# Recurrent stage of a two-block layer: modulation weights in quarter slots with three buffers, and two of the dense weight loads asked for at other places

## What is computed

```
sh1, sc1, ga1, sh2, sc2, ga2 = adaln(c, w_mod[i], b_mod[i])        # silu(c) @ w_mod + b
px = modulate(rms_norm(x, norm_mix[i]), sh1, sc1) @ w_in[i]
pc = modulate(rms_norm(xc, norm_mix[i]), csh1, csc1) @ w_in[i]
yc_rw, s_ctx = rwkv_mix(rwkv_streams(conv3(pc[..., :RW_COLS], ...)), (s_zero, s_zero), ...)
yx_rw, _ = rwkv_mix(rwkv_streams(conv3(px[..., :RW_COLS], ...)), s_ctx, ...)
yx = concat([yx_rw, short_conv_mix(px, ...), fourier_mix(px)]) @ w_out[i]
```

## Time and profile before

| | us |
|---|---|
| median of 3 runs | 3565.4 |
| lowest and highest | 3557.53, 3569.54 |
| the profiled execution, its time | 3560.43 |
| the profiled execution, its span | 3558.3 |
| PE busy | 3416.1 (96%) |
| DVE busy | 2336.2 (66%) |
| ACT busy | 564.6 (16%) |

### The profile page before, as it was taken

One profiled execution on the slowest core, in us unless ns is written; L12 is line 12 of the kernel. 1 busy time (PEld: TensorE's weight loads), 2 busy tenths in 40 slices (PEclk: granted clock), 3 DMA queues, 4 the chain that ended last, 5 costly groups with the idle time before them and its releaser, 6 DMA issues. The chain is left out here.

```text
span 3558.3 us, 58548 instructions
## 1 busy us (share of the span) xinstructions
PE 3416.1 (96%) x25037; PEld 2754.3 (77%) x25037; DVE 2336.2 (66%) x4471; ACT 564.6 (16%) x1072; POOL 162.9 (5%) x168
## 2 busy tenths in 40 slices
PE   7998899999999999999999999999999999999999
PEld 4455565577778888889998866767877888888888
DVE  2377777885559888998777654555754656644644
ACT  2232222221010000000003133222221000000000
POOL 1000000000000000000001000000001000000000
PEclk9999999999999999999999999999999999999999
DMA  9833323353686888776674734544324676654543
GB/s 338 259 91 100 103 81 106 106 140 105 210 284 223 260 260 260 244 245 204 196 232 160 229 125 142 166 142 157 103 73 148 221 233 201 222 174 161 178 166 130
DMA packets 663410, 638.48 MB, mean 179 GB/s; under 512 B 43490, under 2 KB 630752, under 8 KB 662128
## 3 DMA queue, kind: packets, MB, share of 16 engines
q1 hardware_dynamic: 554464, 563.16, 49.3%
q10 hardware_dynamic: 108016, 71.44, 6.9%
q0 software_dynamic: 672, 0.15, 0.0%
HBM read 628.41 MB, written 6.29 MB: 178 GB/s over the span
## 5 line engine op out<-in xcount | busy, mean ns | idle before, releaser
L2005 PE MATMUL bank<-work,extra 128*128 128x256 f32 x2112 | 463.0, 379 | 0.0
L664 DVE SCALAR_TENSOR_TENSOR work<-weight_ring,silu_c,work 128x256 f32<-128x256 f32 x1050 | 450.5, 502 | 0.0
L2005 PEld LDWEIGHTS bank<-work,extra 128*128 128x128 f32 x2112 | 400.7, 190 | 54.1
L2005 PE MATMUL bank<-weight_ring,work 128*128 128x256 f32 x1408 | 316.7, 383 | 7.8 <-ACT work L2138 7.5
L2206 DVE TENSOR_TENSOR work<-weight_ring 128x2048 f32<-128x2048 f32 (+2 forms) x72 | 129.6, 1800 | 293.1 <-DMA weight_ring<-in_w_gate_up 168.2
L2005 PEld LDWEIGHTS bank<-weight_ring,work 128*128 128x128 f32 x1408 | 268.4, 192 | 45.3 <-issue 8.3
L1013 PE MATMUL bank<-work,x_channels 128*128 128x256 f32 (+1 forms) x704 | 243.5, 486 | 0.0
L2752 PE MATMUL bank<-work,weight_ring 128*128 128x512 f32 x448 | 203.9, 600 | 1.2 <-PEq L2448 1.2
L1013 PEld LDWEIGHTS bank<-work,x_channels 128*128 128x128 f32 x704 | 129.3, 194 | 75.6 <-issue 63.5
L2005 PE MATMUL bank<-weight_ring,extra 128*128 128x256 f32 x704 | 159.4, 379 | 3.5 <-DVE extra L2201 3.5
L2005 PE MATMUL bank<-work 128*128 128x256 f32 x704 | 159.2, 379 | 0.0
(11 more groups left out here) (463 smaller groups left out, 5477.9 us busy)
## 6 DMA issues: line engine op xcount, KB each, us to landing
weight_ring<-in_w_mod SPq DMA_DIRECT2D x80, 2048.0 KB, 9.9
weight_ring<-in_w_gate_up SPq DMA_DIRECT2D x44, 2048.0 KB, 9.3
weight_ring<-in_w_in SPq DMA_DIRECT2D x26, 2048.0 KB, 9.5
weight_ring<-in_w_gate SPq DMA_DIRECT2D x22, 2048.0 KB, 8.3
weight_ring<-in_w_up SPq DMA_DIRECT2D x22, 2048.0 KB, 13.3
weight_ring<-in_w_down SPq DMA_DIRECT2D x20, 2048.0 KB, 8.1
weight_ring<-in_w_mod ACTq DMA_DIRECT2D x32, 1024.0 KB, 6.4
weight_ring<-in_w_out SPq DMA_DIRECT2D x16, 2048.0 KB, 9.6
```

Source lines behind the costliest of these rows:

```text
L664: ins = v_.scalar_tensor_tensor(a, w[:, k, :], c, a, ALU.mult, ALU.add)
L2005: last = mm(product(u, p), right[p][:, k, :], left[p][:, k, :], start=k == 0, stop=k == 7)
```

## The change

- The one buffer `mod_half` (8 steps) becomes three buffers `mod_part` of 4 steps (512 KB): two in the place of the old one, the third in the tile `work`. `load_part(n)` asks for a quarter slot as soon as DVE is done with the part three before it. A unit has eight parts. ACT asks for parts 2 and 3 of a unit after it has taken out x0, part 4 after the decays, part 5 after the last solve result (`w_out`), 6 and 7 after PE's `read_rows`, and the next unit's 0 and 1 at the end of the unit.
- The dense weights that ACT asked for after `w_out` (by the first `dense_out` behind it) are asked for before the `w_out` copies, inside the solve.
- `dense_out` at the first place of the chain (`marks[hp, 0]`, `n == 0`) no longer asks for weights. ACT then waits for `r_mm` (the end of `read_rows`) and asks for them there, ahead of parts 6 and 7.

```
-    mod_half = take("slot2", 2048).rearrange("p (k c) -> p k c", k=KT // 2)
+    mod_part = [take("slot2", 4, 256) for _ in range(2)]
...
+    mod_part.append(take("work", 4, 256))
...
-            def dense_out(upto):
+            def dense_out(upto, fetch=True):
...
-                    load(LOADS_UPTO[j + 1] + WBUFS)
+                    if fetch:
+                        load(LOADS_UPTO[j + 1] + WBUFS)
...
-            def load_half(n):
-                W("mod_step", KT // 2 * n)
-                c0 = (MOD_FIRST + n // 2) * 256
-                act.dma_start(mod_half, st.dram["w_mod"][n % 2 * 1024:n % 2 * 1024 + 1024, c0:c0 + 256].rearrange("(t p) n -> p t n", p=P)
-                              ).then_inc(S("mod_half_in"), 16)
+            def load_part(n):
+                W("mod_step", 4 * (n - 2))
+                k0, c0 = n % 4 * 4 * P, (MOD_FIRST + n // 4) * 256
+                act.dma_start(mod_part[n % 3], st.dram["w_mod"][k0:k0 + 4 * P, c0:c0 + 256].rearrange("(t p) n -> p t n", p=P)
+                              ).then_inc(S(f"mod_in{n % 3}"), 16)
...
-                load_half(4 * hp + 1)
+                load_part(8 * hp + 2)
+                load_part(8 * hp + 3)
...
+                load_part(8 * hp + 4)
                 if hp:
                     squares(hp - 1)
...
                 dense_out(marks[hp, "round"] - 1)
+                W("dense_mm", marks[hp, "round"])
+                load(LOADS_UPTO[marks[hp, "round"]] + WBUFS)
                 for tp in range(2):
                     W("w_mm", 2 * hp + tp + 1)
...
-                load_half(4 * hp + 2)
+                load_part(8 * hp + 5)
                 dense_out(marks[hp, "gram"])
                 for n in range(14):
-                    dense_out(marks[hp, n])
-                    if n == 1:
-                        load_half(4 * hp + 3)
+                    dense_out(marks[hp, n], n > 0)
+                    if n == 0:
+                        W("r_mm", hp + 1)
+                        load(LOADS_UPTO[n_out] + WBUFS)
+                        load_part(8 * hp + 6)
+                        load_part(8 * hp + 7)
                 dense_out(marks[hp, "end"])
                 if more:
-                    load_half(4 * hp + 4)
+                    load_part(8 * hp + 8)
+                    load_part(8 * hp + 9)
```

More of the change, by code:

```diff
@@ L1398, in dense_out @@
                     n_out += 1
-            def load_half(n):
-                W("mod_step", KT // 2 * n)
-                c0 = (MOD_FIRST + n // 2) * 256
-                act.dma_start(mod_half, st.dram["w_mod"][n % 2 * 1024:n % 2 * 1024 + 1024, c0:c0 + 256].rearrange("(t p) n -> p t n", p=P)
-                              ).then_inc(S("mod_half_in"), 16)
+            def load_part(n):
[3 more added lines that the diff above has]
+                              ).then_inc(S(f"mod_in{n % 3}"), 16)
             load(WBUFS)
-            load_half(0)
+            load_part(0)
+            load_part(1)
             def key_squares(hp):
@@ L1662, in head_norm, with mod_macs @@
                 v_.tensor_tensor(st.yr[:, hp, :], bank[4][:, T:2 * T], yn, ALU.mult).then_inc(S("y_gated"), 1)
-            def mod_macs(half, steps):
-                slot = half // 2
-                acc = mod_acc[:, slot % MOD_GROUP, :]
+            def mod_macs(part, steps=range(4)):
+                acc = mod_acc[:, part // 4 % MOD_GROUP, :]
                 if 0 in steps:
-                    W("mod_half_in", 16 * (half + 1))
+                    W(f"mod_in{part % 3}", 16 * (part // 3 + 1))
                 for k in steps:
-                    kc = half % 2 * (KT // 2) + k
+                    kc = part % 4 * 4 + k
                     x = st.silu_c[:, kc:kc + 1]
                     if kc == 0:
-                        ins = v_.tensor_scalar(acc, mod_half[:, k, :], x, None, ALU.mult)
+                        ins = v_.tensor_scalar(acc, mod_part[part % 3][:, k, :], x, None, ALU.mult)
                     else:
-                        W("mod_step", half * (KT // 2) + k)
-                        ins = v_.scalar_tensor_tensor(acc, mod_half[:, k, :], x, acc, ALU.mult, ALU.add)
+                        W("mod_step", 4 * part + k)
+                        ins = v_.scalar_tensor_tensor(acc, mod_part[part % 3][:, k, :], x, acc, ALU.mult, ALU.add)
                     ins.then_inc(S("mod_step"), 1)
-            whole = range(KT // 2)
             unit_keys(0)
@@ L1693, in _ @@
                     W("dense_mm", DENSE.index(("modsum", hp - 1)) + 1)
-                mod_macs(4 * hp, whole)
+                mod_macs(8 * hp)
+                mod_macs(8 * hp + 1)
                 W("gr_mm", hp + 1)
@@ L1707, in _ @@
                         v_.tensor_tensor(x, bank[tp + 2 * d][:].rearrange("p (a b) -> p a b", a=4), x, ALU.add).then_inc(S("z_add"), 1)
-                mod_macs(4 * hp + 1, whole)
+                mod_macs(8 * hp + 2)
+                mod_macs(8 * hp + 3)
                 if more:
@@ L1725, in _ @@
                     if tp == 0:
-                        mod_macs(4 * hp + 2, whole)
+                        mod_macs(8 * hp + 4)
+                        mod_macs(8 * hp + 5)
                 W("r_mm", hp + 1)
@@ L1740, in _ @@
                     if n in MOD_CHAIN:
-                        mod_macs(4 * hp + 3, range(n - MOD_CHAIN[0], n - MOD_CHAIN[0] + 1))
+                        i = n - MOD_CHAIN[0]
+                        mod_macs(8 * hp + 6 + i // 4, range(i % 4, i % 4 + 1))
                     if n >= 2:
```

## The result

| | before | after |
|---|---|---|
| median of 20 runs each, us | 3564.94 | 3575.50 |
| lowest and highest, us | 3557.53, 3584.53 | 3561.72, 3587.53 |
| profiled execution: its time, its span, us | 3560.43, 3558.3 | 3578.16, 3576.4 |
| mean granted clock of the profiled execution | 0.987 | 0.981 |

The ratio after to before is 1.0025, with an interval from 1.0016 to 1.0034: the changed kernel is 10.6 us slower by its medians, 17.7 us by the two profiled executions. The forecast was 3560 us.

The account below looks back on a forecast made before the run. The prediction took PE, the busiest engine, to bound the kernel, so only its stand-stills could come back. Terms of -11.8, +8.5 and 0 summed to -3.3 us, set against a mean of 3563.2: 3560 us, eight-in-ten range 3545 to 3574.

Parts of the forecast that it names:

- What bounds the kernel, and what "issue" is: PE is busiest, so only its stand-stills can come back; "issue" gaps in the transitions are each one late instruction packet.
- the smallest gap that the prediction took: Transitions: 1.9 us taken to stay of a gap, since matmuls use up a packet faster than one is fetched.
- Part 1: Transitions of units 0 to 6: less load there shortens PE's gaps and a wait for ACT, -11.8 us.
- the danger that was named with 0 to 1 us: The load in the solve can delay the packet fetched just before the transitions, 0 to 1 us a unit, 0 taken.
- The upper bound of part 1: All gaps of units 0 to 6 to zero, 17.7 us with the ACT wait.
- Part 2: Chain step 6, units 1 to 5: modulation parts land later behind two dense loads, +8.5 us (5.0 to 11.5).
- the two ways of reckoning: Landing of unit 2's chain part, at 3.5 or 4.4 us per further MB: 473.8 or 475.1.
- Part 3: The rest: five more DMA issues a unit on ACT, four-step slots, dense loads moved; 0, at most 3 us in all.
- PE already waits there, so it is lost one for one: Chain step 6: each microsecond of longer wait costs PE one, 1.7 us a unit in five units.
- The parts come in time: Faster rival, chance 0.27: parts land before chain step 6, DVE's and PE's waits go, -19.5 us, 3544 us.
- The burst decides (slower): Slower rival, chance 0.14: chain loads land in turn, +3.6 us a unit, part 1 halved, 3575; decides from 2.3 a unit.
- The fetches are late all the same: Rival, chance 0.05: SP's small blocks keep the transition gaps, sum +8.5 us at most, 3571 us.

Follow-up runs that it names:

- sp_later: parts_first with SP's stream of the next stage's weights started behind PE's first transition half of unit 7; 3536.41 us, ratio 0.9925.
- sp_after_both: parts_first with SP's stream of the next stage's weights started behind PE's second transition half of unit 7; 3532.53 us, ratio 0.9903.
- quarters_only: The changed kernel with the dense loads where they were before, so the quarter slots alone; 3553.09 us, ratio 0.9974.
- no_solve_load: The changed kernel without the dense load inside the solve, which goes back to the first dense_out behind w_out; 3575.76 us, ratio 1.0037.
- parts_no_solve: parts_first without the dense load inside the solve, which goes back to the first dense_out behind w_out; 3545.02 us, ratio 0.9943.
- dense_only: The kernel before with the two dense loads moved as in the change and the halves of modulation weights kept; 3584.10 us, ratio 1.0064.
- dose_one_12: parts_first with twelve small DVE operations added at chain step 6 of units 0 to 5, no DMA changed; 3578.04 us, ratio 1.0044.
- parts_first: The changed kernel with parts 6 and 7 asked for ahead of the dense loads behind the read rows; 3535.73 us, ratio 0.9927.
- the first experiments: quarters_only, dense_only, no_solve_load and parts_first, beside which the kernel before had a median of 3563.36 us.
- dose_one_6: parts_first with six small DVE operations added at chain step 6 of units 0 to 5, no DMA changed; 3545.84 us, ratio 0.9951.

## Why the prediction was wrong

**What bounds the kernel, and what "issue" is: right.** The gaps went where the load went, in the changed kernel and in sp_later and sp_after_both. In unit 2 of the changed kernel the packet of the instruction queue is seen once between 444.2 and 445.5, and PE goes on at 446.56, again some 1.3 us after its end:

```profile
q1 hardware_dynamic: 500, 0.03, 30.8%
q8 instruction: 1, 0.02, 4.5%
```

No packet of q10 is in this stretch, and still 1.99 us are lost: the smallest gap that the prediction took, 1.9, was the right size (1.93 to 1.99 in units 1, 2, 3 and 6, 1.70 in unit 5).

**Part 1, -11.8: the terms right within 0.5 us, the sum less.** Unit 2: 3.05 and 2.44 (3.1 and 2.4 predicted); unit 3: 2.91 (2.9); unit 1: 0.55 (0.6); unit 6: 0.82 (0.9); unit 0: 1.59 for the gap before the fill (1.1) and 0.57 for ACT's (0.8, with DVE's masks next, as it was put). That is 11.9. Against it stand gaps put at nothing, above all the 1.53 us before 635.39 in unit 4. Over the stage "issue" fell by 9.3 us. The gap in unit 4 lies at the packet before the transitions, the danger that was named with 0 to 1 us, and it took the place of a wait of 1.01 us for DVE, so it lost 0.5. The four kernels without the load inside the solve do not have it (before, quarters_only, no_solve_load, parts_no_solve), and of the nine with that load seven do. That points to the load; why dense_only and sp_later are without it stays open. The upper bound of part 1 was added up wrongly: the gaps of units 0 to 6 in the earlier trace rows, with the wait for ACT, make 23.2 us and not 17.7. The outcome didn't come near either.

**Part 2, +8.5: right in kind, at its upper bound.** The wait in step 6 grew by 2.04 us in unit 1, 2.33, 2.20, 2.13 and 2.26 in units 2 to 5: 11.0, where 5.0 to 11.5 was the range. Two dense loads and a part took 12.6 us from the first issue; the two ways of reckoning gave 11.2 and 12.5. Unit 0, taken as 0, lost 1.15. All in all the chain's idle time rose by 11.8.

**Part 3, 0:** nothing speaks against it. DVE and ACT are busy as before, and what else PE waits for fell by about 3 us.

So the sum of the waits was -3.3 by the prediction and is -0.6 by the trace. The step that failed is the sentence in part 2 "PE already waits there, so it is lost one for one". The waits of 1.2 to 1.35 us in units 2 to 5 became 3.4 to 3.7, and around or just behind stand-stills of that length the clock fell to half for 10 to 14 us. dose_one_12 makes such stand-stills without a late load and has such falls, of 3.4 to 13.7 us. The 17.4 us of PE's longer busy time have no term in the sum, and no rival had one either. The Trainium skill (TensorE: Matmul & The Clock Gate, HAM oscillation — how this bites in real kernels) tells of matmul loops that fall to half rate at the waits between their rounds; these traces agree, for single waits some 95 us apart. With the measured waits, -0.6, this makes +16.8, and the stage is 16.3 longer; with the forecast's own -3.3 it would have been +14.1. The row that should have given the warning stood in the earlier trace rows: PEclk 0.83 behind the 5.04 us gap. It was read as part of the scene and not as a price. The same price has a good side, which was missed as well: with the shorter gaps in units 2 and 3 there is less half clock at the transitions (before: 3.4 us behind each gap of unit 2, 6.8 in unit 3; after: 3.4 and none). parts_first has both the shorter gaps and no late parts: against the kernel before its stage has 19.2 us less idle time, PE is busy 7.1 us less, and the medians differ by 27.6 us.

The size in single runs follows the clock too. The 20 runs of the changed kernel have a mean granted clock of 0.980 to 0.985, and a straight line through them gives 3.1 us for each 0.001; the 22 runs of the kernel before beside the first experiments have 0.983 to 0.988, with a median of 0.986 to the changed kernel's 0.9825. That is 10.9 us for 0.0035; the changed kernel's median is 10.6 us over that of the 20 runs of the kernel before and 12.1 over that of these 22. So the profiled execution's 17.7 is on the high side, and the clock term is worth less than 17 us on average.

**The rivals.** *The parts come in time* did not happen: two loads stood ahead of them. parts_first shows that the rival's gain was there by another order of issues: 19.2 us less idle time, where the rival had 19.5, and the clock's part on top. *The burst decides (slower)* gave 3575 us, and 3575.5 was measured, but not for its reason: its part was to land 13.8 us after the first issue, and landed after 12.6; its price of 3.6 us a unit was 2.2, just short of the 2.3 at which it was to decide; and part 1 did not come out at half its size. The third issue in a row did hold ACT, 3.82 us, and nothing waited for ACT there. *The fetches are late all the same* is refuted by the gaps of units 2 and 3.

What stays open: why a wait of about 2 us in unit 1 was followed by half clock in the changed kernel and not in no_solve_load, what brings the clock down in unit 0, and the cause of the new gap in unit 4. The first in rows, 378 to 392 us, just behind that wait, changed kernel and then no_solve_load:

```profile
378.00:392.00 14.00, 13.38 (x178) 10.20 (x180) 8.76 (x33) 1.98 (x5) 0.00 (x0) 0.64 0.40 114
```
```profile
378.00:392.00 14.00, 13.38 (x231) 10.02 (x229) 11.42 (x45) 3.71 (x9) 0.00 (x0) 1.00 0.52 152
```

## What to carry to other kernels

When a change makes a stand-still of TensorE longer, price it twice: the wait, and the stretch behind it at half clock; look at PEclk behind the longest waits that the trace already has, and at what one matmul takes there. The same twelve operations cost 14.9 us when they make waits of up to 1 us and 42.3 us when they make waits of 3.65 and more. Where loads share a queue, ask first for what is needed first: here the order of four issues was worth more than the size of the slots or the place of the dense loads.

## What the runs showed of the hardware that was not expected

- Lone stand-stills of 3.42 to 3.75 us in the chain, in a stage in which PE is busy to 91%, went with 3.4 to 13.7 us at 1.2 GHz, mostly 10. In some units the clock fell up to 2 us before PE went on, in others up to 1.3 us behind that; in unit 2 PE was then busy without a gap at half clock. Waits of 1.31 us in dose_one_6 were not followed by it, the 1.35 us in unit 2 of the kernel before by 3.4 us of it, and those of about 2 us were in one kernel and not in the other. In unit 0 of dose_one_6, 2.59 us went with PEclk 0.50 from 287 to 297 us, but that place has half clock in every kernel of this case.
- A fetch of instructions costs 1.2 to 2.0 us in a dense row of 32x64 matmuls where no large load is under way (1.99 in unit 2 of the changed kernel, 1.23 and 1.87 in unit 7 of sp_after_both), 2.1 to 3.2 us in units 2 and 3 of no_solve_load, where 1.5 MB are asked for just before, and 4.3 to 5.0 with 2 MB or more (5.04 in unit 2 of the kernel before, 4.90 in sp_later, 4.34 in unit 7 of quarters_only). The Trainium skill (Runtime: NRT & Kernel Launch, Instruction fetch mechanics) calls the crossing of a block mostly hidden; all kernels of this case contradict it at this place.
- An issue can hold its engine for microseconds when other loads are under way. Behind two of 1 MB (0.37 and 1.79 us to issue) the third took 3.82: issue at 462.29, free at 466.11, first landing at 466.0. It isn't the count of loads: in unit 1 of parts_first, behind two parts of 512 KB, the third issue, of 1 MB, took 0.53 us, and the fourth 5.14, until 368.49; the second part landed at 368.6. In both, 2 MB stood ahead of the issue that was held.
